# Block 2's heads: VectorE writes only the columns that change, and a head's norm is inverted with tokens in partitions

## The chip, the cores and the metric

The kernel runs as one program on one core of a Trainium2 chip. The metric is the device time of one execution in microseconds (us). Everything is computed in 32-bit floats. The engines are TensorE (PE in the views), VectorE (DVE), ScalarE (ACT) and SyncE (SP), which issues the weight transfers. Each runs its own instructions in order, and they wait for one another by semaphores.

## The reference

Two transformer blocks of width 2048 run over 256 tokens. The change is in the second block's two recurrent mixers, each with eight heads of width 128, over a chunked sequence of 512 tokens (256 context, 256 grid) in both directions:

```python
# _hgrn2, a gated linear attention, per head:
f = lb + (1.0 - lb) * jax.nn.sigmoid(fz);  key = (1.0 - lb) * jax.nn.sigmoid(-fz)
diff = bc[..., :, None, :] - bc[..., None, :, :]      # bc: running sum of log f
att = jnp.einsum('bhtk,bhsk,bhtsk->bhts', qc, kc, exp(diff) below the diagonal)
# _gated_deltanet, per head: a unit lower triangular system is solved
a = eye + jnp.where(strict, (kb @ kc.T) * decay, 0.0)
# both, per head, after the two directions are added:
o = _rmsnorm_2(o_f + _flip(o_b), norm_w) * gate
```

The root-mean-square norm of the last line runs over the 128 features of a token.

## The kernel before

Each mixer is a chain of eight heads. A head consists of a start, two strands (r = 0 forward, r = 1 backward) and an end, which adds the strands' outputs, takes the norm and applies the gate. Every part is written three times, as a generator for TensorE, VectorE and ScalarE, and each `yield` ends a phase. `lockstep` advances the strands together, so that all three engines run through the same phases; a head has 58 phases. The end of a head runs in the first phases of the next one. The chain of the forget heads (`forget_*`, names `hg`) starts eight phases after that of the delta heads (`delta_*`, names `dn`). `beside` spreads a background over these phases: eight groups of a projection whose matmuls (L592) keep TensorE busy. The order of each engine's instructions is therefore fixed by hand.

Both strands build a 128x128 triangular matrix out of seven levels. At level l the tokens lie in blocks of 2 x half with half = 128 >> (l + 1), and a level joins the first half of each block with the second.

- In `forget_vector` a level subtracts the running sums from their middle value (L1597 for first halves, L1598 for second ones), ScalarE takes the exponential of the whole 128x256 tile (L1654), VectorE multiplies by keys and queries (L1602, L1603), TensorE multiplies (L1510), and `copy_predicated` takes the masked elements of the 128x256 product over into `att` (L1608). Before the levels, the keys are a product (L1546) followed by one with a column (L1549).
- In `delta_vector` a level masks the matrix `nt` into `mt` (L1795, 128x512 for four token tiles). TensorE multiplies (L1710), ScalarE copies (L1847), TensorE multiplies the halves (L1717, L1719), and VectorE subtracts them in place (L1803, L1805, half-columns only).
- In a new delta head, `delta_tensor` writes rows of gates into banks 0 to 3 (L1685, L1687); L1767 on VectorE reads them. Bank 1 is also the one in which the end of the head before sums its squares (L1955).
- An end adds and squares (L1970 to L1972), TensorE sums the squares over the features with a matrix of ones (L1955), so that each token's sum stands in all 128 partitions; then the mean (L1975), the root on ScalarE (L1986), the reciprocal (L1978) and two products (L1979, L1980) are all 128x256.

Of the kernel before, what the change touches and what calls it, by code (L numbers as in the profile page):

```python
# [13 lines left out]
P = 128  # L14
# [234 lines left out]
class Kernel:  # L249
# [4 lines left out]
    def __init__(self, nc, io, known, pofs, cofs):  # L254
# [25 lines left out]
        self.arena = sb("arena", ARENA)  # L280
        masks = self.c("masks").rearrange("p (r l t) -> p r l t", r=2, l=7)
# [20 lines left out]
    def places(self):  # L302
# [47 lines left out]
        for r in range(2):  # L350
            self.hg.append(dict(f=a.take(4, P), k=a.take(4, P), e1=a.take(4, P), cum=a.take(4, P + 2), ks=a.take(4, P),
                                att=a.take(2, P), qe=a.take(2, P), lev=a.take(2, P), st=a.take(P), eend=a.take(4)))
        self.hvf, self.hvt = a.take(4, P), a.take(4, P)
        self.hq, self.hgt = ([a.take(2, P) for _ in range(2)] for _ in range(2))
# [8 lines left out]
        self.dzg = [self.mix[:, 3, :], self.mix[:, 4, :]]  # L363
        assert a.at <= ARENA - 1024, a.at
# [1116 lines left out]
def level_halves(x, half):  # L1481
    t = x.rearrange("p j (b two n) -> p j b two n", two=2, n=half)
    return t[:, :, :, 0, :], t[:, :, :, 1, :]
# [42 lines left out]
def forget_vector(k, r, head):  # L1526
# [62 lines left out]
    for level in range(7):  # L1589
        half = P >> (level + 1)  # L1590
        nb = P // (2 * half)
        mid = cm[:, 0:2, 0:P].rearrange("p j (b n) -> p j b n", n=2 * half)[:, :, :, half:half + 1].broadcast_to((P, 2, nb, half))
        c0, c1 = level_halves((after if fwd else before)[:, 0:2, :], half)
        m0, m1 = level_halves(m, half)
        k0, k1 = level_halves(kk[:, 0:2, :], half)
        q0, q1 = level_halves(k.hq[head % 2], half)
# [9 lines left out]
        mask = k.masks[r][:, level, :].unsqueeze(1).broadcast_to((P, 2, P)).bitcast(U32)  # L1606
# [14 lines left out]
def forget_scalar(k, r, head):  # L1621
# [51 lines left out]
def delta_tensor(k, r, head):  # L1673
# [7 lines left out]
    if head:  # L1681
        pe.wait_ge(*s.at("dn_o_mean", head - 1))
# [23 lines left out]
    for level in range(5, -1, -1):  # L1706
        yield
        pe.wait_ge(*s.at(*ev("masked", level)))
        for j in range(NT):
            mm = pe.matmul(b0[:, P * j:P * j + P], mt[:, j, :], x[:, j, :], start=True, stop=True)  # L1710
# [35 lines left out]
def delta_vector(k, r, head):  # L1746
# [15 lines left out]
    yield  # L1762
    yield
    yield
# [60 lines left out]
def delta_scalar(k, r, head):  # L1825
# [3 lines left out]
    yield  # L1829
    yield  # L1830
    yield
    yield
# [117 lines left out]
def end_tensor(k, name, head):  # L1950

    pe, s = k.nc.tensor, k.s
    bank, sq = (k.acc[3], k.hsq) if name == "hg" else (k.bank[1], k.dsq)
    pe.wait_ge(*s.at(name + "_o_sq", head))
    pe.matmul(bank[:, 0:T], k.c("ones"), sq, start=True, stop=True).then_inc(*s.made("tensor_done", name + "_o_sum", head))  # L1955
    yield
    yield

def end_vector(k, name, head):
# [15 lines left out]
    v.tensor_scalar(sq, bank[:, 0:T], 1.0 / P, 1e-6, ALU.mult, ALU.add).then_inc(*s.made("vector_done", name + "_o_mean", head))  # L1975
    yield
    v.wait_ge(*s.at(name + "_o_root", head))
    serial(k, v.reciprocal(sq, sq))  # L1978
    serial(k, v.scalar_tensor_tensor(o, o, w, sq, ALU.mult, ALU.mult))  # L1979
    v.tensor_tensor(dst, o, gate, ALU.mult).then_inc(*s.made("vector_done", name + "_end", head))  # L1980

def end_scalar(k, name, head):
    a, s, sq = k.nc.scalar, k.s, k.hsq if name == "hg" else k.dsq
    yield
    a.wait_ge(*s.at(name + "_o_mean", head))
    a.activation(sq, sq, ACT.Sqrt).then_inc(*s.made("scalar_done", name + "_o_root", head))  # L1986
# [24 lines left out]
def heads2_vector(k):  # L2011
# [12 lines left out]
    v.memset(k.ones_row, 1.0).then_inc(*s.made("vector_done"))  # L2024
    for r in range(2):
# [471 lines left out]
```

## Time and profile before

| what | value |
|---|---|
| median of 3 runs | 4655.85 us (4651.43 to 4659.77) |
| span of the profiled execution | 4650.0 us |
| block 2's heads in it | 2403 to 3284 us |
| busy in the span: TensorE, VectorE, ScalarE | 4321.8, 2756.5, 1602.9 us |
| mean granted TensorE clock | 0.961 |

### The profile page before, as it was taken

The numbers are of one execution on the slowest core, as the hardware profiler recorded it, in microseconds if no ns is written. First come the engines' busy times: TensorE is split into PE (matmuls) and PEld (weight loads), VectorE is DVE, ScalarE is ACT, GpSimd is POOL, SyncE is SP. The second block draws the span as 40 slices with busy tenths as digits, with TensorE's granted clock in tenths as the row PEclk, the third lists the DMA queues.
The fourth block names the chain that finished last, engine by engine and source line by source line (L and its number), as shares of the span: only waits on it lengthen the run. The fifth ranks groups of instructions, "written<-read, shape, count | busy, mean of one in ns | idle before, by whom it ended". The sixth has DMA issues, their size and how long they took to land.

```text
span 4650.0 us, 69801 instructions
## 1 busy us (share of the span) xinstructions
PE 4321.8 (93%) x28096; PEld 3686.2 (79%) x28096; DVE 2756.5 (59%) x5537; ACT 1602.9 (34%) x2841; POOL 0.2 (0%) x4
## 2 busy tenths in 40 slices
PE   8989997899999989999988989888899998999998
PEld 8433334899999978889778888888655898999998
DVE  5666664576566542234558877777533666655654
ACT  4121112454444432234123333333100444444443
POOL 0000000000000000000000000000000000000000
PEclk9989998999999999999899999999988999999999
DMA  6744454466666544457451222121522654656653
GB/s 187 246 138 143 143 173 135 151 187 190 187 182 190 187 134 123 115 144 212 128 156 56 60 65 62 54 65 46 156 76 77 200 190 131 191 187 186 186 189 129
DMA packets 383296, 669.52 MB, mean 144 GB/s; under 512 B 44009, under 2 KB 77642, under 8 KB 382460
## 3 DMA queue, kind: packets, MB, share of 16 engines
q1 hardware_dynamic: 329280, 597.83, 42.8%
q10 hardware_dynamic: 53692, 67.22, 4.4%
q8 instruction: 221, 3.62, 0.3%
q14 instruction: 103, 0.84, 0.1%
HBM read 634.87 MB, written 29.46 MB: 143 GB/s over the span
## 4 chain that ended last, share of the span: by engine, by line
PE 64%; DVE 13%; ACT 3%; issue 3%; DMA 1%; ACTq 0%; DVEq 0%
PE acc L550 13%; PE acc L552 13%; PE acc L551 13%; PE acc L592 8%; PE bank L550 2%; PE bank L552 2%; PE bank L551 2%; ACT weights_hi L514 1%; PE bank L2193 1%; PE bank L1719 1%; PE bank L1710 1%; PE bank L1717 1%; DVE arena L1544 1%; PE acc L1510 1%; DVE arena L676 1%
## 5 line engine op out<-in xcount | busy, mean ns | idle before, releaser
L529 DVE TENSOR_TENSOR weights_lo<-weights_ring,weights_hi 128x512 fp32r<-128x512 f32 x1600 | 1093.6, 691 | 1019.4 <-ACT weights_hi L514 1017.7
L514 ACT ACTIVATE weights_hi<-weights_ring 128x512 fp32r<-128x512 f32 x1600 | 992.8, 629 | 1076.4 <-PE acc L552 879.9
L551 PE MATMUL acc<-arena_halves,weights_hi 128*128 128x256 f32 (+2 forms) x3136 | 914.2, 292 | 0.0
L550 PE MATMUL acc<-arena_halves,weights_lo 128*128 128x256 f32 (+1 forms) x2944 | 861.6, 293 | 21.2 <-DVE weights_lo L529 12.3
L552 PE MATMUL acc<-arena_halves,weights_hi 128*128 128x256 f32 (+1 forms) x2944 | 859.9, 292 | 0.0
L550 PE MATMUL acc<-moving_halves,weights_lo 128*128 128x256 f32 (+1 forms) x2816 | 790.4, 281 | 68.4 <-DVE weights_lo L529 67.8
L552 PE MATMUL acc<-moving_halves,weights_hi 128*128 128x256 f32 (+1 forms) x2816 | 785.1, 279 | 0.0
L551 PE MATMUL acc<-moving_halves,weights_hi 128*128 128x256 f32 x2624 | 729.7, 278 | 0.0
L592 PE MATMUL acc<-moving,weights_ring 128*128 128x256 f32 x2304 | 588.1, 401 | 21.8 <-ACT arena L695 11.1
L551 PEld LDWEIGHTS acc<-arena_halves,weights_hi 128*128 128x128 f32 x3136 | 590.1, 188 | 13.5
L550 PEld LDWEIGHTS acc<-moving_halves,weights_lo 128*128 128x128 f32 x2816 | 533.7, 190 | 76.8 <-DVE weights_lo L529 48.9
L550 PEld LDWEIGHTS acc<-arena_halves,weights_lo 128*128 128x128 f32 x2944 | 553.5, 188 | 34.3 <-DVE weights_lo L529 13.1
L552 PEld LDWEIGHTS acc<-arena_halves,weights_hi 128*128 128x128 f32 x2944 | 554.1, 188 | 14.2
L552 PEld LDWEIGHTS acc<-moving_halves,weights_hi 128*128 128x128 f32 x2816 | 533.6, 189 | 0.0
L592 PEld LDWEIGHTS acc<-moving,weights_ring 128*128 128x128 f32 x2304 | 444.3, 202 | 108.3 <-issue 37.6
L551 PEld LDWEIGHTS acc<-moving_halves,weights_hi 128*128 128x128 f32 x2624 | 496.8, 189 | 0.0
L1144 PE MATMUL acc<-weights_ring,cc 128*2 128x512 f32 x768 | 352.0, 600 | 2.8 <-DMA weights_ring<-in_w_ada 2.8
L1144 PEld LDWEIGHTS acc<-weights_ring,cc 128*2 128x2 f32 x768 | 56.9, 85 | 238.3 <-issue 225.3
L551 PE MATMUL bank<-arena_halves,weights_hi 128*128 128x256 f32 (+2 forms) x640 | 208.0, 325 | 0.0
L550 PE MATMUL bank<-arena_halves,weights_lo 128*128 128x512 f32 (+1 forms) x512 | 172.3, 337 | 0.0
L552 PE MATMUL bank<-arena_halves,weights_hi 128*128 128x512 f32 (+1 forms) x512 | 171.8, 336 | 0.0
L1710 PE MATMUL bank<-arena 128*128 128x128 f32 x768 | 113.0, 302 | 28.9 <-DVE arena L1795 28.7
(422 smaller groups left out, 4815.5 us busy)
## 6 DMA issues: line engine op xcount, KB each, us to landing
weights_ring<-in_w_in SPq DMA_DIRECT2D x624, 256.0 KB, 2.7
weights_ring<-in_w_ff SPq DMA_DIRECT2D x512, 256.0 KB, 3.0
weights_ring<-in_w_ada SPq DMA_DIRECT2D x384, 256.0 KB, 3.0
weights_ring<-in_w_up SPq DMA_DIRECT2D x256, 256.0 KB, 3.0
weights_ring<-in_w_down SPq DMA_DIRECT2D x256, 256.0 KB, 3.2
weights_ring<-in_w_out SPq DMA_DIRECT2D x128, 256.0 KB, 3.2
weights_ring<-in_w_branch SPq DMA_DIRECT2D x96, 256.0 KB, 3.3
s_state<-arena ACTq DMA_DIRECT2D x36, 256.0 KB, 3.0
```

The lines of the kernel that those rows point to most:

```text
L514: a.activation(whi, k.slot(g.ring0 + kc), ACT.Copy).then_inc(*s.made("scalar_done", "high", n))
L529: v.tensor_tensor(wlo, k.slot(g.ring0 + kc), whi.bitcast(F32), ALU.subtract).then_inc(*s.made("vector_done", "low", n))
L550: pe.matmul(g.out[m], wlo[:, cols], xhi, start=first, stop=False, skip_group_check=g.shared)
L551: pe.matmul(g.out[m], whi[:, cols], xlo, start=False, stop=False, skip_group_check=g.shared)
L552: mm = pe.matmul(g.out[m], whi[:, cols], xhi, start=False, stop=last, skip_group_check=g.shared)
L592: mm = pe.matmul(g.out[m], k.slot(g.ring0 + kc)[:, m * P:(m + 1) * P], g.x(kc), start=kc == 0 and m % 2 == 0, stop=last, skip_group_check= ...
L676: v.tensor_scalar(tmp, g.out[m], 0.0, None, ALU.max, ALU.bypass).then_inc(*s.made("vector_done", "relu", g.name, g.index, m))
L1144: mm = pe.matmul(g.out[0], ccv[:, kc, :], k.slot(g.ring0 + kc), start=kc == 0, stop=kc == g.kchunks - 1)
L1510: mm = pe.matmul(po[:, P * j:P * j + P], h["lev"][:, j, :], h["lev"][:, j, :], start=True, stop=True)
L1544: own(v.reciprocal(f[:, j, :], f[:, j, :]))
L1710: mm = pe.matmul(b0[:, P * j:P * j + P], mt[:, j, :], x[:, j, :], start=True, stop=True)
L1717: pe.matmul(b0[:, 64 * j:64 * j + 64], xt[:, j, :], level_columns(y[:, j, :], level, r), start=True, stop=True)
```

## The change

- Delta masks: levels 5 to 0 each get a tile of their own (`mts`, twelve in all, for both strands), zeroed once by a memset, and the product with the mask writes only the columns that the mask can set: 128x256 instead of 128x512. Seven of the tiles are new memory (`level_own`, zeroed at the program's start), five lie in a buffer that is free in this stage (`level_mix`, zeroed just before the heads).
- Forget levels: both halves of a block are subtracted in one instruction, both are multiplied in one (`keys_and_queries` views keys and queries as one operand, for which the query buffers were moved), the sign goes into ScalarE's exponential, which is now one instruction for each half, and the predicated copy takes only the half-columns that can change.
- Keys: the column goes into the first product.
- Norm: the sum of squares is taken with the tokens in partitions, as one column for each token tile; mean, root and reciprocal are 128x2; then VectorE makes a diagonal matrix of them and TensorE spreads it to all partitions (`o_spread`), from where the first product reads it in the bank. An end has a phase more.
- `delta_tensor` therefore waits in all heads but the first for the end of the head before (`dn_end`) instead of for its mean, and the delta strands of these heads start one phase later.

```diff
+        self.level_own = sb("level_masks", 7, 512)
...
+            if r:
+                self.hq_at = a.at
+                self.hq = [a.take(2, P) for _ in range(2)]
...
+        self.o_cols = {"hg": a.take(2), "dn": a.take(2)}
...
+        self.level_mix = [self.mix[:, 5 + 2 * i:7 + 2 * i, :].rearrange("p a b -> p (a b)") for i in range(5)]
...
+    v.memset(k.level_own[:, :, :], 0.0).then_inc(*s.made("vector_done"))
...
+def half_columns(x, half):
+
+    t = x.rearrange("p j t -> p (j t)").rearrange("p (c two n) -> p two c n", two=2, n=half)
+    return t, t[:, 0, :, :], t[:, 1, :, :]
+
+def keys_and_queries(k, r, head, half):
+
+    keys, queries = k.hg[r]["k_at"], k.hq_at + 2 * P * (head % 2)
+    first, second = (keys, queries + half) if r == 0 else (queries, keys + half)
+    apart = second - first
+    t = k.arena[:, first:first + 2 * apart].rearrange("p (two d) -> p two d", two=2)[:, :, 0:2 * P]
+    return t.rearrange("p two (c q n) -> p two c q n", q=2, n=half)[:, :, :, 0, :]
+
+def of_second(x, half, second):
+    return x.rearrange("p j (b two n) -> p j b two n", two=2, n=half)[:, :, :, second, :]
...
-    own(v.tensor_tensor(kk, e1, f, ALU.mult))
+    own(v.scalar_tensor_tensor(kk, e1, lb1c, f, ALU.mult, ALU.mult))
...
-    own(v.tensor_scalar(kk, kk, lb1c, None, ALU.mult, ALU.bypass))
...
-        own(v.tensor_tensor(m0, mid, c0, ALU.subtract))
-        own(v.tensor_tensor(m1, c1, mid, ALU.subtract), *ev("spans", level))
+        both, m0, m1 = half_columns(m, half)
+        own(v.tensor_tensor(blocks(m), blocks(sums), mid, ALU.subtract), *ev("spans", level))
...
-        own(v.tensor_tensor(m0, m0, k0 if fwd else q0, ALU.mult))
-        own(v.tensor_tensor(m1, m1, q1 if fwd else k1, ALU.mult), *ev("level", level))
+        own(v.tensor_tensor(both, both, keys_and_queries(k, r, head, half), ALU.mult), *ev("level", level))
...
-        own(v.copy_predicated(att, mask, tiles(po, 2)), *(ev("att") if level == 6 else ()))
+        own(v.copy_predicated(of_second(att, half, 1 - r), mask, of_second(tiles(po, 2), half, 1 - r)), *(ev("att") if level == 6 else ()))
...
-        a.activation(h["lev"], h["lev"], ACT.Exp).then_inc(*s.made("scalar_done", *ev("span_decays", level)))
+        _, m0, m1 = half_columns(h["lev"], P >> (level + 1))
+        a.activation(m0, m0, ACT.Exp, scale=-1.0).then_inc(*s.made("scalar_done"))
+        a.activation(m1, m1, ACT.Exp).then_inc(*s.made("scalar_done", *ev("span_decays", level)))
...
     if head:
-        pe.wait_ge(*s.at("dn_o_mean", head - 1))
+        yield
+        pe.wait_ge(*s.at("dn_end", head - 1))
...
-        own(v.tensor_tensor(mt, nt, k.masks[r][:, level, :].unsqueeze(1).broadcast_to((P, NT, P)), ALU.mult), *ev("masked", level))
+        mask = level_columns(k.masks[r][:, level, :], level, 1 - r).unsqueeze(1).broadcast_to((P, NT, 1 << level, half))
+        own(v.tensor_tensor(of_second(d["mts"][level], half, 1 - r), of_second(nt, half, 1 - r), mask, ALU.mult), *ev("masked", level))
...
-    pe.matmul(bank[:, 0:T], k.c("ones"), sq, start=True, stop=True).then_inc(*s.made("tensor_done", name + "_o_sum", head))
-    yield
+    for j in range(2):
+        mm = pe.matmul(bank[:, j:j + 1], sq[:, P * j:P * j + P], k.c("ones")[:, 0:1], start=True, stop=True)
+    mm.then_inc(*s.made("tensor_done", name + "_o_sum", head))
+    yield
+    yield
+    pe.wait_ge(*s.at(name + "_o_diagonal", head))
+    for j in range(2):
+        mm = pe.matmul(bank[:, P * j:P * j + P], k.c("ones"), sq[:, P * j:P * j + P], start=True, stop=True)
+    mm.then_inc(*s.made("tensor_done", name + "_o_spread", head))
...
-    serial(k, v.reciprocal(sq, sq))
-    serial(k, v.scalar_tensor_tensor(o, o, w, sq, ALU.mult, ALU.mult))
+    serial(k, v.reciprocal(col, col))
+    v.tensor_tensor(sq.rearrange("p (j t) -> p j t", j=2), k.ident.unsqueeze(1).broadcast_to((P, 2, P)),
+                    col.unsqueeze(2).broadcast_to((P, 2, P)), ALU.mult).then_inc(*s.made("vector_done", name + "_o_diagonal", head))
+    yield
+    v.wait_ge(*s.at(name + "_o_spread", head))
+    serial(k, v.scalar_tensor_tensor(o, o, w, bank[:, 0:T], ALU.mult, ALU.mult))
...
+    for part in k.level_mix:
+        v.memset(part, 0.0).then_inc(*s.made("vector_done"))
...
-        nc = bacc.Bacc("TRN2", target_bir_lowering=False, num_devices=1)
+        nc = bacc.Bacc("TRN2", target_bir_lowering=False, num_devices=1, dynamic_dma_scratch_size=2048)
```

## Rows read from the trace of the kernel before

**Rows 1.** Busy time by stretch: the heads, then the two halves of one head.
```profile
core 0: us, PE busy (x) PEld busy (x) DVE busy (x) ACT busy (x) POOL busy (x), PEclk, DMA share, GB/s
2403.00:3284.00 881.00, 778.45 (x5226) 717.72 (x5227) 692.15 (x1792) 307.06 (x617) 0.00 (x0) 0.93 0.21 61
2628.00:2663.00 35.00, 28.40 (x193) 25.34 (x191) 33.99 (x65) 12.38 (x21) 0.00 (x0) 0.94 0.11 31
2664.00:2695.00 31.00, 31.00 (x224) 29.77 (x222) 21.77 (x57) 10.53 (x21) 0.00 (x0) 0.91 0.24 68
```
**Rows 2.** Chain that ended last, in the heads: start us, us, engine, line.
```profile
2429.12 0.69 DVE arena L1795
...
2443.21 0.40 DVE arena L1549
...
2507.26 0.44 DVE arena L1608
...
2535.03 1.76 DVE arena L1978
...
2663.42 3.79 PE bank L1710 x16
...
2675.32 1.79 PE bank L1710 x16
...
3204.92 0.71 DVE arena L1795
...
3264.00 0.48 DVE arena L1608 x2
...
3277.12 1.76 DVE arena L1978
```
**Rows 3.** Groups of VectorE in the heads: count, busy us, mean ns, idle before.
```profile
L1795 DVE TENSOR_TENSOR arena<-arena,consts_sb 128x512 f32<-128x512 f32 x96 | 66.4, 692 | 3.3
...
L1805 DVE TENSOR_TENSOR arena<-arena,bank 128x256 f32<-128x256 f32 x96 | 39.8, 415 | 11.0 <-PE bank L1719 11.0
...
L1549 DVE TENSOR_SCALAR arena<-arena 128x512 f32<-128x512 f32 x16 | 7.7, 480 | 0.0
...
L1979 DVE SCALAR_TENSOR_TENSOR mixed<-mixed,params_sb 128x256 f32<-128x256 f32 x8 | 3.9, 485 | 0.3
```
**Rows 4.** Timeline of VectorE where instructions follow one another: start, us.
```profile
2567.34 0.42 DVE L1581 TENSOR_TENSOR arena<-arena 128x256 f32<-128x256 f32 x1
2567.68 0.99 DVE L1585 TENSOR_TENSOR arena<-arena 128x256 f32<-128x256 f32 x2
...
2571.19 0.28 DVE L1597 TENSOR_TENSOR arena<-arena 128x128 f32<-128x128 f32 x1
2571.39 0.28 DVE L1598 TENSOR_TENSOR arena<-arena 128x128 f32<-128x128 f32 x1
```
**Rows 5.** Chain at the boundary of two delta heads, twice.
```profile
2620.08 0.34 DVE mixed L1975
...
2620.47 2.07 PE bank L1685 x8
...
2625.51 0.89 PE bank L1687 x8
...
2728.56 0.34 DVE mixed L1975
...
2733.74 1.04 DVE arena L1767 x4
```
**Rows 6.** Groups of ScalarE and VectorE that price the new small instructions.
```profile
L1654 ACT ACTIVATE arena<-arena 128x256 f32<-128x256 f32 x112 | 43.3, 413 | 99.5 <-DVE arena L1598 99.5
...
L1770 DVE TENSOR_TENSOR arena<-arena 128x4 f32<-128x4 f32 x16 | 2.6, 162 | 0.6
...
L2252 DVE MEMSET arena<- 1x512 f32 x4 | 1.9, 485 | 0.6 <-DVE arena L2250 0.6
```
**Rows 7.** Timeline: VectorE's first instruction of the program.
```profile
25.61 0.44 DVE L749 TENSOR_SCALAR rstd<-bank 128x272 f32<-128x272 f32 x1 [25.61 <-PE bank L742]
```

More of the change, by code:

```diff
@@ L363, in places @@
         self.dzg = [self.mix[:, 3, :], self.mix[:, 4, :]]
+        self.level_mix = [self.mix[:, 5 + 2 * i:7 + 2 * i, :].rearrange("p a b -> p (a b)") for i in range(5)]
+        mt = [self.level_own[:, i, :] for i in range(7)] + self.level_mix
+        for r in range(2):
+            self.dn[r]["mts"] = [mt[6 * r + level].rearrange("p (j t) -> p j t", j=4) for level in range(6)]
         assert a.at <= ARENA - 1024, a.at
@@ L1479, in hg_views @@
     return h, cm[:, :, 1:P + 1], cm[:, :, 0:P], cm[:, :, P:P + 1]
-def level_halves(x, half):
-    t = x.rearrange("p j (b two n) -> p j b two n", two=2, n=half)
-    return t[:, :, :, 0, :], t[:, :, :, 1, :]
+def half_columns(x, half):
[9 more added lines that the diff above has]
+    return x.rearrange("p j (b two n) -> p j b two n", two=2, n=half)[:, :, :, second, :]
 def forget_tensor(k, r, head):
@@ L1591, in forget_vector @@
         nb = P // (2 * half)
[L1592 to L1596, printed above, removed]
-        own(v.tensor_tensor(m0, mid, c0, ALU.subtract))
-        own(v.tensor_tensor(m1, c1, mid, ALU.subtract), *ev("spans", level))
+        blocks = lambda x: x.rearrange("p j (b n) -> p j b n", n=2 * half)
+        mid = blocks(cm[:, 0:2, 0:P])[:, :, :, half:half + 1].broadcast_to((P, 2, nb, 2 * half))
+        sums = (after if fwd else before)[:, 0:2, :]
+        both, m0, m1 = half_columns(m, half)
+        own(v.tensor_tensor(blocks(m), blocks(sums), mid, ALU.subtract), *ev("spans", level))
         yield
@@ L1709, in delta_tensor @@
         for j in range(NT):
-            mm = pe.matmul(b0[:, P * j:P * j + P], mt[:, j, :], x[:, j, :], start=True, stop=True)
+            mm = pe.matmul(b0[:, P * j:P * j + P], d["mts"][level][:, j, :], x[:, j, :], start=True, stop=True)
         mm.then_inc(*s.made("tensor_done", *ev("left", level)))
@@ L1761, in delta_vector @@
     own(copy(k, mt, col(be)), *ev("spread"))
-    yield
-    yield
-    yield
+    for _ in range(4 if head else 3):
+        yield
     v.wait_ge(*s.at(*ev("rows")))
@@ L1794, in delta_vector @@
         v.wait_ge(*own.last)
-        own(v.tensor_tensor(mt, nt, k.masks[r][:, level, :].unsqueeze(1).broadcast_to((P, NT, P)), ALU.mult), *ev("masked", level))
+        half = P >> (level + 1)
+        mask = level_columns(k.masks[r][:, level, :], level, 1 - r).unsqueeze(1).broadcast_to((P, NT, 1 << level, half))
+        own(v.tensor_tensor(of_second(d["mts"][level], half, 1 - r), of_second(nt, half, 1 - r), mask, ALU.mult), *ev("masked", level))
         yield
@@ L1828, in delta_scalar @@
     ev = lambda name, *x: ("dn_" + name, r, head, *x)
[L1829 to L1832, printed above, removed]
+    for _ in range(5 if head else 4):
+        yield
     a.wait_ge(*s.at(*ev("logs")))
@@ L1974, in end_vector @@
     v.wait_ge(*s.at(name + "_o_sum", head))
-    v.tensor_scalar(sq, bank[:, 0:T], 1.0 / P, 1e-6, ALU.mult, ALU.add).then_inc(*s.made("vector_done", name + "_o_mean", head))
+    col = k.o_cols[name]
+    v.tensor_scalar(col, bank[:, 0:2], 1.0 / P, 1e-6, ALU.mult, ALU.add).then_inc(*s.made("vector_done", name + "_o_mean", head))
     yield
     v.wait_ge(*s.at(name + "_o_root", head))
-    serial(k, v.reciprocal(sq, sq))
-    serial(k, v.scalar_tensor_tensor(o, o, w, sq, ALU.mult, ALU.mult))
+    serial(k, v.reciprocal(col, col))
+    v.tensor_tensor(sq.rearrange("p (j t) -> p j t", j=2), k.ident.unsqueeze(1).broadcast_to((P, 2, P)),
+                    col.unsqueeze(2).broadcast_to((P, 2, P)), ALU.mult).then_inc(*s.made("vector_done", name + "_o_diagonal", head))
+    yield
+    v.wait_ge(*s.at(name + "_o_spread", head))
+    serial(k, v.scalar_tensor_tensor(o, o, w, bank[:, 0:T], ALU.mult, ALU.mult))
     v.tensor_tensor(dst, o, gate, ALU.mult).then_inc(*s.made("vector_done", name + "_end", head))
 def end_scalar(k, name, head):
-    a, s, sq = k.nc.scalar, k.s, k.hsq if name == "hg" else k.dsq
+    a, s, col = k.nc.scalar, k.s, k.o_cols[name]
     yield
     a.wait_ge(*s.at(name + "_o_mean", head))
-    a.activation(sq, sq, ACT.Sqrt).then_inc(*s.made("scalar_done", name + "_o_root", head))
+    a.activation(col, col, ACT.Sqrt).then_inc(*s.made("scalar_done", name + "_o_root", head))
     yield
```

6 lines of the change are left out of this document (3 added, 3 removed).

## The prediction

> **What bounds the kernel now.** I read the time by stretch first, then the chain that ended last, then the groups of VectorE instructions, then the timeline where one head follows another. Block 2's heads take 881 of the 4650 us, and in them the granted TensorE clock is lower than 1 on average [rows 1]. The reader should see two halves in a head. In 2628 to 2663 VectorE is busy 33.99 of 35 us and TensorE 28.40. In 2664 to 2695 TensorE is busy all of the time and VectorE 21.77 of 31 us [rows 1]. The chain says the same: in the first half each VectorE instruction stands behind the one before, from 2663.42 on TensorE's matmuls follow one another [rows 2]. Added up over the 1892 pieces of the whole stage, from which [rows 2] are taken, the chain has 372 us of VectorE, 445 us of TensorE and 27 us of ScalarE. So a VectorE instruction made shorter pays where the chain runs over it, and nowhere else. TensorE's own work in its half is untouched.
>
> **The price of a VectorE instruction.** On the chain a following, independent instruction starts before the one ahead has ended: two 128x128 products of 0.28 us start 0.20 us apart, two of 128x256 start 0.34 us apart (2567.34 and 2567.68) [rows 4]. So two of 128x128 merged into one of 128x256 save 0.40 - 0.34 = 0.06 us of the engine, not 2 x 0.28 - 0.42 = 0.14. One of 128x512 cut to 128x256 saves 0.69 - 0.42 = 0.27 us, waited for or not [rows 3, 4]. Strides don't cost: L1805 reads and writes the same half-columns, of every level, at 415 ns [rows 3].
>
> **Part 1, delta masks (L1795).** 96 products of 128x512 become 128x256. The chain runs over 52 of them (34.0 us, first and last in [rows 2]). 52 x 0.27 = 14.0 us saved. The other 44 lie beside TensorE's work: 0.
>
> **Part 2, keys (L1549).** All 16 lie on the chain from 2443.21 on, 0.40 us each, by pace and not by their duration of 480 ns [rows 2, 3]. The product that takes the column in has a scalar read from memory; L1979, with such a scalar, takes 485 ns for 256 columns, L1581 without it 0.42 us [rows 3, 4]. 16 x 0.34 = 5.4 us saved.
>
> **Part 3, the levels of the forget heads.** 112 levels: two subtractions and two products each merge, and the predicated copy (L1608) goes from 256 to 128 columns. The copies on the chain are 17 pieces, about 24 copies, in 7.4 us [rows 2]; the halved one I put at 0.31 (0.44 less the 0.14 that lies between 0.28 and 0.42 [rows 4]): 24 x 0.13 = 3.2 us. About eight merged pairs on the chain give 0.06 each, 0.5 us. ScalarE's exponential goes from one of 128x256 (413 ns [rows 6]) to two of 128x128. Bounds from its rows: nothing more, or a second full 413 ns. Its back-to-back starts are closer than its durations, as on VectorE, so I take 0.10 us. It lies on the chain four times: 0.4 us lost. Elsewhere ScalarE, busy a third of the stage [rows 1], hides it; were that cover gone, 112 x 0.10 = 11 us. Net 3.3 us.
>
> The Trainium skill, page Advanced Engine Details and Errata, section The Read-Write Bubble, says that on ScalarE and VectorE latency stands exposed between instructions, so that many small ones cost more than one large one. It speaks for the merged pairs and against the split exponential. [rows 4] show for VectorE that part of that latency is overlapped when nothing is waited for. By the rule taken fully, merging would save 0.14 and splitting lose about 0.2 us, and on these few places of the chain the sum would move by under 1 us.
>
> **Part 4, the norm.** 16 ends. Removed: a 1.76 us reciprocal and a 0.34 us mean of 128x256, and 0.2 us of ScalarE's root. Added: the same on 128x2 (a 128x4 instruction takes 0.16 us [rows 6]), a 128x256 product with the identity (0.42), and a trip to TensorE and back. For the forget ends the trip has a phase of other VectorE work over it; nothing waits at once for that end. The chain runs over five of their reciprocals. Gross 1.76 + 0.34 + 0.42 - 0.16 - 0.2 - 0.2 - 0.36 = 1.6 us. In the middle heads ScalarE's table loads and copies, and L1717 behind them, follow within about 1.5 us, so I take 1.0; the last two ends, with nothing else to run, are priced with their matmuls at 0.9 each. 4 x 1.0 + 2 x 0.9, and a few tenths for the others: 6.5 us.
>
> **Part 5, the boundary between delta heads.** TensorE must write the new head's rows (L1685, L1687) into the bank in which the norm now lives for longer: it waits for the head's end instead of the mean. Queued behind that wait are everything else on TensorE, background projection too. VectorE waits for the rows at L1767. Before, the rows ran under the reciprocal. From the mean's start to the second strand's L1767: 2728.56 to 2733.74, 5.2 us, at full clock; 2620.08 to 2626.40, 6.3 us, with the rows at half clock [rows 5]. After: mean 0.16, root 0.2, reciprocal 0.2, diagonal 0.42, two matmuls 0.6 (four follow one another in 0.89 at 2625.51, and the first has its fill of some 0.15 before it), two products 0.48 and 0.42, handovers 0.3: 2.8 us, and only then the rows, 3.7 us at full clock, 5.9 as at 2620.47, 7.2 if all of it runs at half clock. So 6.5, 8.7 or 10.0 us: a loss of 1.3, 2.4 or 3.7 us for each of seven boundaries. In this trace three were fast and four slow. I take 3 x 1.3 + 4 x 2.4 = 14 us lost, bounds 9 (all fast) and 26 (all at half clock). The reciprocal's saving is already in it.
>
> **Part 6, the rest.** Five memsets of 128x512 come before the first head, where VectorE has just been released by ScalarE and the first rows wait for it. A 512-column memset took 485 ns [rows 6]: 2.4 us lost. The large memset at the program's start lies under the 25.61 us in which VectorE first waits for TensorE [rows 7]: 0. Extra matmuls, 0.4 us for each of 16 ends, fall where TensorE has room: 0, or 7 us if not. The moved buffers and the DMA scratch size add no instruction: 0.
>
> **Sum.** 14.0 + 5.4 + 3.3 + 6.5 = 29 us saved; 14 + 2.4 = 16 us lost. Net 13 us: the profiled span of 4650.0 becomes 4637. The median of the runs, 4655.85, is 5.9 above that span, so 4643. A difference under 0.2%, 9 us, can hardly be told from none.
>
> **Rivals.**
> - *A, the clock comes back.* At a mean grant of 0.93, with levels of 1.2 and 2.4 GHz, about 14% of the stage, 123 us, runs at half clock. At 2663.42 sixteen records take 3.79 us instead of 1.79 [rows 2], right after a stretch in which TensorE was idle. A shorter first half packs TensorE's same work denser. If most such dips vanish, up to 25 us more: 4643 - 25 = 4618, with fast boundaries 4613. Against it: a new idle place at the boundary. The Trainium skill, page TensorE: Matmul & The Clock Gate, section Part 1, says that activity releases the throttle; these rows agree.
> - *B, what is saved is given back.* TensorE, at 81% in 2628 to 2663 [rows 1], or ScalarE becomes the one waited for, so that half of part 1 is lost (7 us), or all boundaries run at half clock (12 us more). That gives 4650 or 4655, both together 4662: no change.
> - *C, slower by the boundary.* TensorE now idles at two places within some 6 us: before the spreading matmuls and before the rows. If that leaves it at half clock in every boundary and on through the next products, the loss is 3.7 us of part 5 and the dearer matmuls up to L1703, another 3 us: 6.7 x 7 = 47 us against 29 - 2.4 = 27 saved, 4676. It decides from a loss of 36 / 7 = 5.1 us a boundary. For it: four of seven boundaries are already slow. Against: after the rows VectorE sets the pace, under which slow matmuls are partly hidden.
>
> **Chances.** Forecast (4630 to 4655) 0.46, A 0.24, B 0.19, C 0.11. Taking the part of the forecast and of B under 4646.5 as faster: faster 0.61, same 0.28, slower 0.11. The range leaves out the ends of A and most of C: 4612 to 4662.
>
> **What would show it.** L1795's successor at 0.42 us and fewer of its pieces on the chain; the small reciprocal near 0.2 us; TensorE idle for 2 to 3 us before each later L1685, and VectorE idle for 1 to 2 us before L1767; a first half of a head some 4 us shorter and a second half unchanged. I'm wrong if the level steps of TensorE's half get shorter too, if ScalarE's split exponentials come on to the chain, or if the mean clock of the stage moves by more than 0.02.

## The result: slower by 0.9%

The kernel after takes 4698.15 us (median of 4 runs, 4685.42 to 4705.38), beside 4653.64 us for the kernel before in the same series (4 runs). The ratio is 1.0088, 95% interval 1.0068 to 1.0108. The forecast was 4643 us. The profiled execution has a span of 4704.0 us (before 4650.0) and a mean granted clock of 0.957 (before 0.961). One execution of e13 (below) took 8939.64 us at a mean granted clock of 0.632 and is left out of every comparison.

Busy time by stretch, kernel after. Start and end, length, then busy us of TensorE, its weight loads, VectorE, ScalarE and GpSimd, each with its count, the granted clock, DMA:

```profile
0.00:2403.00 2403.00, 2258.75 (x13612) 1798.63 (x13612) 1295.54 (x2405) 802.64 (x1356) 0.20 (x4) 0.97 0.55 165
2403.00:3330.00 927.00, 792.61 (x5320) 731.80 (x5321) 620.05 (x1573) 314.60 (x732) 0.00 (x0) 0.92 0.21 59
```

The heads now end at about 3327 us and not 3280. That is 47 of the 54 us between the two spans. The rest of the program takes 1377 us in this execution and took 1370 before; in the other kernels' profiled executions, which don't change it, it takes 1369 to 1378. VectorE's busy time in the stage fell from 692 us [rows 1] to 620: the work was taken away as planned. Added up over the chain that ended last in the stage, VectorE's part fell from 372 to 319 us, and TensorE's rose from 440 (the prediction has 445) to 545. What left one engine's account came back, and more, on the other's.

Groups of VectorE in the heads, kernel after (count, busy us, mean ns of one, idle before and its releaser). The first two lines answer to L1795 in [rows 3], the last is the product that took in L1549; L1825 is the other half of the pair whose second is L1805 there:

```profile
L1817 DVE TENSOR_TENSOR level_masks<-arena,consts_sb 128x256 f32<-128x256 f32 x56 | 23.8, 425 | 1.9
L1817 DVE TENSOR_TENSOR mixed<-arena,consts_sb 128x256 f32<-128x256 f32 x40 | 17.0, 425 | 1.4
L1621 DVE TENSOR_TENSOR arena<-arena 128x256 f32<-128x256 f32 x112 | 45.4, 424 | 22.1 <-ACT arena L1674 22.1
L1626 DVE COPY_PREDICATED arena<-consts_sb,acc 128x128 f32<-128x128 uint32 x112 | 37.9, 339 | 99.0 <-PE acc L1532 95.1
L1825 DVE TENSOR_TENSOR arena<-arena,bank 128x256 f32<-128x256 f32 x80 | 33.3, 416 | 55.0 <-PE bank L1740 55.0
L1812 DVE TENSOR_TENSOR arena<-consts_sb,bank 128x512 f32<-128x512 f32 x16 | 11.0, 685 | 12.2 <-PE bank L1724 12.1
L1568 DVE SCALAR_TENSOR_TENSOR arena<-arena 128x512 f32<-128x512 f32 x16 | 12.0, 752 | 0.6
```

The mask costs what it was priced at: 425 ns, where 692 was before. The last column, the idle time before the instruction, holds the news. The predicated copy waits 95 us for TensorE (63 before), L1825 55 us (25 for the same form before), and L1812, which waited for nothing before, 12 us. All waits of VectorE for TensorE in the stage sum to 239 us, 141 before.

**The boundary between delta heads** looks as it was forecast for a slow one. Timeline, kernel after, with what each instruction waited for:

```profile
2859.40 0.15 DVE L2003 TENSOR_SCALAR arena<-bank 128x2 f32<-128x2 f32 x1
2860.05 0.42 DVE L2007 TENSOR_TENSOR mixed<-consts_sb,arena 128x256 f32<-128x256 f32 x1
2860.53 1.23 PE L1982 MATMUL bank<-mixed,consts_sb 128*128 128x128 f32 x4 [1.87 <-DVE mixed L2007]
2862.31 0.42 DVE L2012 TENSOR_TENSOR moving<-mixed 128x256 f32<-128x256 f32 x1
2862.79 2.07 PE L1706 MATMUL bank<-consts_sb,arena 128*128 128x128 f32 x8 [0.18 <-DVE moving L2012]
2866.61 1.13 DVE L1787 TENSOR_SCALAR arena<-bank,arena 128x128 f32<-128x128 f32 x4 [3.36 <-PE bank L1708]
2868.39 1.12 DVE L1787 TENSOR_SCALAR arena<-bank,arena 128x128 f32<-128x128 f32 x4 [0.40 <-PE bank L1708]
```

The rows (L1706, L1685 before) start behind the end's last product and run at half clock, 2.07 us for eight records as in [rows 5]. From the mean to the second strand's L1787 it is 9.0 us; the forecast had 8.7 for a boundary whose rows run at half clock. This is the longest of the seven. They take 6.8 to 9.0 us, 8.0 on average, where they took 5.2 to 6.5, 5.7 on average, in the kernel before. So this is a real loss, 16 us in all, but no place for the 47 us by which the heads got longer.

**What lies elsewhere** shows 50 us further on. Timeline, kernel after, level 3 of a delta head:

```profile
2908.42 1.16 PE L1731 MATMUL bank<-arena,mixed 128*128 128x128 f32 x8
2909.78 0.63 ACT L1655 ACTIVATE arena<-arena 128x512 f32<-128x512 f32 x1 [4.67 <-DVE arena L1592]
2911.52 1.06 ACT L1867 ACTIVATE arena<-bank 128x512 f32<-128x512 f32 x2
2912.15 1.10 PE L1738 MATMUL bank<-arena 128*128 128x64 f32 x8 [1.71 <-ACT arena L1867]
2915.47 1.91 PE L1740 MATMUL bank<-arena 128*128 128x64 f32 x8
2917.42 0.42 DVE L1825 TENSOR_TENSOR arena<-arena,bank 128x256 f32<-128x256 f32 x1 [2.02 <-PE bank L1740]
```

ScalarE is idle for 4.67 us, waiting for VectorE's sums in the forget strands (L1655). The delta strands' copy L1867 stands behind it in the same queue; the first strand's matmuls that it reads (L1731) had ended at 2908.5 us, 3 us before the copy starts. TensorE needs that copy and is idle for 1.71 us. VectorE then waits for TensorE. In the kernel after without the shift (e3 below) the order on ScalarE is the other one, and the copies L1866 (L1867 above) wait for their own matmuls alone:

```profile
2877.44 0.60 ACT L1866 ACTIVATE arena<-bank 128x512 f32<-128x512 f32 x1 [2.12 <-PE bank L1730]
2879.14 0.60 ACT L1866 ACTIVATE arena<-bank 128x512 f32<-128x512 f32 x1 [1.11 <-PE bank L1730]
2879.76 1.28 ACT L1655 ACT_TABLE_LOAD   x1
2881.05 0.63 ACT L1655 ACTIVATE arena<-arena 128x512 f32<-128x512 f32 x1
```

And another place, on TensorE:

```profile
2879.73 0.71 PE L1976 MATMUL acc<-consts_sb,arena 128*128 128x1 f32 x4 [3.11 <-DVE arena L1999]
2880.30 1.09 PE L1936 MATMUL acc<-consts_sb,arena 128*128 128x128 f32 x4
2881.18 3.06 PE L1724 MATMUL bank<-consts_sb,arena 128*128 128x128 f32 x16
2883.13 0.69 DVE L1812 TENSOR_TENSOR arena<-consts_sb,bank 128x512 f32<-128x512 f32 x1 [2.17 <-PE bank L1724]
```

The left product of level 6 (L1724, "left 6" from here on) stands behind the sum of squares of a forget head's end (L1976), which waits for VectorE. In the kernel before, and in e3, both (the copy of level 3 and left 6) were ahead of these neighbours. They changed places because the delta strands run one phase later than the forget strands beside them.

The clock falls at both places. Stretches of the kernel after (columns as in the first view, the granted clock is the third number from the end):

```profile
2878.00:2879.70 1.70, 0.00 (x0) 0.00 (x0) 1.63 (x5) 0.00 (x0) 0.00 (x0) 1.00 0.34 125
2881.00:2882.00 1.00, 1.00 (x6) 1.00 (x5) 0.00 (x0) 1.00 (x1) 0.00 (x0) 0.50 0.00 0
2912.00:2913.00 1.00, 0.85 (x8) 0.85 (x8) 0.34 (x1) 0.59 (x2) 0.00 (x0) 1.00 0.00 0
2915.00:2916.00 1.00, 1.00 (x7) 1.00 (x6) 0.40 (x1) 0.00 (x0) 0.00 (x0) 0.50 0.00 0
```

At left 6 TensorE has been idle for 3.11 us and is at half clock (0.50) soon after it starts again: sixteen records of L1724 take 3.06 us, where eight take 1.06 in e3. At level 3 it still runs two groups of eight at full clock after its pause (1.10 us for L1738) and is at half clock from about 2914.3 us on, so that the last eight take 1.91.

Waits in the heads, kernel after (engine and line, what it waited for: us in total, times, longest). The first is the largest of all, but ScalarE has time for it; the other three belong to the two places above:

```profile
ACT arena L1867 <- PE bank L1731: 197.1, 71, 10.0
ACT arena L1655 <- DVE arena L1592: 32.2, 7, 4.7
PE acc L1976 <- DVE arena L1999: 22.6, 8, 4.0
PE bank L1738 <- ACT arena L1867: 11.2, 8, 1.7
```

### The profile page after: what moved, and what is told of

Same layout as the page of the kernel before. It is cut to its first block, busy times and chain, and to the rows that moved or that the text cites. A ratio compares the mean times of both kernels' runs of the same rounds, so it can differ in the third digit from the quotient of the medians.

```text
span 4704.0 us, 69887 instructions
## 1 busy us (share of the span) xinstructions
PE 4344.5 (92%) x28192; PEld 3707.0 (79%) x28192; DVE 2687.4 (57%) x5319; ACT 1609.8 (34%) x2953; POOL 0.2 (0%) x4
## 4 chain that ended last, share of the span: by engine, by line
PE 65%; DVE 12%; ACT 3%; issue 3%; DMA 1%; ACTq 0%; DVEq 0%
PE acc L559 13%; PE acc L561 13%; PE acc L560 13%; PE acc L601 8%; PE bank L560 2%; PE bank L559 2%; PE bank L561 2%; PE bank L1731 1%; ACT weights_hi L523 1%; DVE arena L1566 1%; PE bank L2227 1%; PE bank L1740 1%; PE bank L1738 1%; PE acc L1532 1%; DVE arena L685 1%
## 5 line engine op out<-in xcount | busy, mean ns | idle before, releaser
L560 PEld LDWEIGHTS bank<-arena_halves,weights_hi 128*128 128x128 f32 x640 | 120.3, 188 | 9.6
```

What stands on the lines that cost most here:

```text
L560: pe.matmul(g.out[m], whi[:, cols], xlo, start=False, stop=False, skip_group_check=g.shared)
```

## The experiments

Each ratio is to the kernel before, timed beside it on the same chip, with its 95% interval. "Shift" is the extra phase of the delta strands in heads 1 to 7. "Steps" are mean times between landmarks of a delta head in the timeline of VectorE, over heads 1 to 7. The landmarks are VectorE's first instruction on the first strand's products (L1802), left 6 (L1812) and each level's result (L1827). The "period" is the mean distance of two heads from head 1 to head 7.

### First: which part

**e1_no_norm**: the kernel after with the old norm, the old wait and no shift; what is left are masks, keys, levels, memsets.

```diff
-        yield
-        pe.wait_ge(*s.at("dn_end", head - 1))
+        pe.wait_ge(*s.at("dn_o_mean", head - 1))
```

> The changed kernel with the old norm, the old wait for the head's mean and without the extra phase: only masks, levels, keys and memsets are changed. Theory (the loss of the change is all in the norm's end and in what it moves): parts 1 to 3 give what was forecast, 23 us, less 2.4 for the memsets, so 4653.6 - 20 = 4633 us (4625 to 4642). Rival (the levels themselves cost, by ScalarE's split exponential and the waits for it): 4655 us or more.

0.9967 [0.9953, 0.9981], 4638.3 us beside 4655.1: 15 us saved (9 to 22 by the interval), forecast 20.

**e2_norm_only**: the kernel before with the new norm, its wait and the shift.

> The kernel before with nothing but the new norm, the wait for the head's end and the extra phase. Theory: it carries the whole loss, 44 + 20 = 64 us, so about 4718 us (4700 to 4730). Rival (levels cost): the norm carries only the 7 x 2.5 us of its boundaries, about 4665 us.

1.0135 [1.0117, 1.0154], 4720.7 us, as forecast. All of the loss comes with the norm, its wait and the shift.

**e3_no_shift**: the kernel after; the one edit is that the shift goes (TensorE's `yield` ahead of the wait for `dn_end`, and its counterparts on VectorE and ScalarE). The wait stays.

> The changed kernel without the extra phase of the delta strands (the wait for the head's end stays; the strands of the two chains stand to one another as before). Theory S (the shift puts the delta matmuls L1724 behind the forget end's sum in TensorE's queue, and VectorE waits for them at L1812, and later steps pair up worse): 7 boundaries give back 4 us each, about 4670 us (4660 to 4680). Theory W (the loss is the wait itself: TensorE stands still until the head's end, and the clock with it): no gain, 4690 to 4705 us.

0.9993 [0.998, 1.0007], 4651.8 us. The shift alone turns this into 1.0088: some 44 to 46 us, the whole loss, and more than the 28 us that the expectation gave it. The period is 113.9 us after, 107.6 here and 107.9 before. The wait at left 6 is gone, and that behind the levels is 30 us where it was 25 before and 55 after (L1811 and L1824 here are L1812 and L1825 after):

```profile
L1811 DVE TENSOR_TENSOR arena<-consts_sb,bank 128x512 f32<-128x512 f32 x16 | 10.9, 679 | 0.0
L1824 DVE TENSOR_TENSOR arena<-arena,bank 128x256 f32<-128x256 f32 x80 | 33.0, 412 | 30.4 <-PE bank L1739 30.3
```

**e4_hg_norm**: new norm for the forget heads only; delta heads have the old norm and wait, and no shift.

> The changed kernel with the new norm for the forget heads alone; the delta heads have the old norm, the old wait and no extra phase. Both theories: as without the norm, less 6 us for the reciprocals on the chain, about 4627 us (4620 to 4637). Rival (a trip to TensorE and back costs wherever it stands, since it holds up the matmuls queued behind it): 4640 us or more.

0.9938 [0.9926, 0.995], 4626.8 us: the fastest kernel of the study. Busy time in its heads (columns as above):

```profile
2403.00:3256.00 853.00, 759.77 (x5283) 701.83 (x5284) 625.10 (x1564) 313.70 (x729) 0.00 (x0) 0.96 0.22 64
```

The heads end at 3248 us and not at 3280, and the clock in them is 0.96, not 0.93 [rows 1]. From e1 to e4 the forget heads' norm saves 0.29%, 13 us (11 by the medians). From e4 to e3 the delta heads' norm with its wait costs 0.55%, 25 us, 3.6 us a boundary. The timelines say the same: from the mean to the second strand's rows it is 8.9 us on average in e3 (7.1 to 10.5) and 5.3 in e4 (5.2 to 6.0).

### Second: the shift alone, and where in a head it hurts

**e5_shift_only**: the kernel before with nothing but the shift.

```diff
     if head:
+        yield
         pe.wait_ge(*s.at("dn_o_mean", head - 1))
```

> The kernel before with nothing but the extra phase of the delta strands in heads 1 to 7 (old norm, old wait, old masks). Theory S: the extra phase is what costs, whatever stands around it: e3 against the changed kernel gives 46 us, so about 4700 us (4690 to 4710). Rival P (the phase costs only where it adds to the new norm's trips): under 4670 us.

1.0117 [1.0102, 1.0132], 4710.2 us, 53 us lost. No part of the new arithmetic is needed for the loss.

**e6_delay_nine**: the kernel after, the forget chain starting nine phases after the delta chain, not eight.

```diff
-    chains = [chain(k, "hg", hg_start, forget, end, 8), chain(k, "dn", dn_start, delta, end)]
+    chains = [chain(k, "hg", hg_start, forget, end, 9), chain(k, "dn", dn_start, delta, end)]
```

> The changed kernel with the forget chain nine phases behind the delta chain instead of eight, so that from head 1 on both chains stand to one another as before the change; the extra phase of the delta strands stays. Theory S1 (the pairing of the two chains' steps in one phase is what costs): the 46 us come back, 4650 to 4660 us. Rival S2 (the phase is lost inside the delta chain itself, between its end and its rows): no gain, 4690 to 4705 us.

0.9975 [0.9966, 0.9984], 4642.7 us. The shift is still there, and the loss is gone, and the steps to left 6 and from level 3 to level 2 are 6.7 and 8.2 us, as in e3 (6.7 and 8.3). So the loss lies in how the steps of the two chains pair up, not in a phase more.

The next four runs are the kernel after with the extra phase at another place. **e7_shift_early** gives the phase back before left 6; **e8_shift_late** begins it there; **e9_shift_level_five** begins it behind left 6; **e10_shift_level_two** behind level 3. For e10, on each engine:

```diff
+        if head and level == 2:
+            yield
```

> The changed kernel, where the delta strands give their extra phase back before the first inverse step: rows, decays and products stand one phase later, all levels stand where they did. Theory S1 with the pairing of the levels and of L1724 behind the forget end's sum as the cost: 4650 to 4660 us. If the pairing of rows and products with the forget chain's last steps costs instead: 4690 us or more. In between: both.

1.0008 [0.9999, 1.0017]: the levels stand where they did, and nearly all of the loss is gone.

> The complement: no extra phase at the rows, but one before the first inverse step, so that only that step and the levels stand one phase later. If the levels' pairing costs: about 4690 to 4700 us. If the rows' and products' pairing costs: 4650 to 4660 us.

1.0112 [1.0099, 1.0125]: all of the loss.

> As the late shift (4709), but the extra phase stands after the first inverse step, so that this step (L1724) is again ahead of the forget end's sum in TensorE's queue and only levels 5 to 0 come one phase later. The landmarks of the traces put 2.3 us a head on that step and 4 to 5 us on the levels. Theory Q (three separate queue orders add up): 4709 - 7 x 2.3 = 4693 us (4685 to 4700). Rival (it all hangs on that first step, the rest follows from its delay): 4650 to 4660 us.

1.0095 [1.0082, 1.0109], 4696 us: nearly all of it, as the theory of separate queue orders had it.

> The extra phase stands between levels 3 and 2, so that ScalarE's copy of level 3 is issued where it was without a shift, ahead of the forget strands' exponential of their sums (which waits for VectorE's scans), and only levels 2 to 0 and the end come later. Theory Q: 4652 us as without any shift, plus up to 1 us a head for the last levels: 4650 to 4662 us. Rival (any extra phase anywhere costs about 7 us a head): 4700 us.

1.0014 [1.0005, 1.0023]. Beside e3 (0.9993), a phase later costs some 7 us for the rows and products at the start of a head (e7; the intervals of e7 and e3 still meet), and some 10 for levels 2 to 0 (e10). Nearly all of the loss comes up between left 6 and level 3. The places don't add up exactly: begun at left 6 (e8) the shift costs more than begun at the start.

**e16_shift_level_three** was run later, with the phase between levels 4 and 3.

> The kernel after with the extra phase given between level 4 and level 3 of the delta strands and not at their start. With the phase before level 5 it took 1.0095 of the kernel before, with the phase behind level 3 only 1.0014. Queue theory (ScalarE's copy of level 3 behind the exponential of sums is the largest place): most of the 38 us between these two, at least 22 us, is still there: 1.006 to 1.009, 4680 to 4694. Rival, the loss is spread evenly over the levels 5, 4 and 3 that run in other phases: two thirds of it go: about 1.004, 4670.

1.0071 [1.0056, 1.0086]. From e16 to e10 is 0.57%, 27 us: level 3 alone. Levels 5 and 4 have 11 us (e9 to e16) and left 6 about 8 (e8 to e9), but for both the intervals of the two runs meet. "Spread evenly" is out.

The steps show where the time goes (us; the step from level 2 to level 1 is 8.4 in all of them):

| step | e3, no shift | after | e9 | e16 | e13 (below) |
|---|---|---|---|---|---|
| products to left 6 | 6.7 | 8.8 | 6.7 | 6.7 | 9.2 |
| left 6 to level 5 | 11.4 | 13.2 | 13.8 | 11.4 | 13.3 |
| level 5 to 4 | 10.4 | 10.2 | 10.1 | 10.4 | 10.0 |
| level 4 to 3 | 8.9 | 8.3 | 8.7 | 11.8 | 7.5 |
| level 3 to 2 | 8.3 | 11.7 | 12.3 | 9.2 | 8.4 |
| level 1 to 0 | 6.1 | 7.1 | 7.1 | 7.1 | 7.1 |

In e9 left 6 has its old place and its old 6.7 us, and yet e9 is no faster than the kernel after (1.0095 beside 1.0088): the next step and the one behind level 3 got longer in its place. So the 2 us a head at left 6 can't be counted as a part of the loss that comes back by itself.

### Third: small checks

**e11_masks_only**: masks on half columns and the memsets, on the kernel before.

> The kernel before with the delta masks on half the columns and the memsets, nothing else of the change. By the prediction's parts 1 and 6: 14.0 - 2.4 = 11.6 us saved, 4644 us (4638 to 4650). Rival (what parts 2 and 3 brought is the whole gain of e1, 16 us, and TensorE sets the pace under the masks): 4652 us or more.

0.9981 [0.9972, 0.9991]: 9 us saved (4 to 13 by the interval, which holds the forecast 11.6).

**e12_hg_norm_delay_nine**: e4 with a delay of nine.

> The fastest kernel so far (new norm for the forget heads alone, 4627) with the forget chain nine phases behind instead of eight: the opposite misalignment of that which cost 46 us. Theory Q (queue orders at three places, each on one side only): the delta steps stand further ahead of the forget steps, so nothing of that kind arises, 4622 to 4637 us. Rival (the eight phases are a tuned optimum, and a step to either side costs): 4650 us or more.

0.9984 [0.9975, 0.9994], 4643.0 us; by the ratios 0.46%, 21 us, more than e4 (16 by the medians, which were taken on two chips). A step to the other side costs too. Which pair it is was not found: its head is slower in several small steps.

### Fourth: the queues themselves

**e13_sums_exp_later**: the kernel after, shift kept. ScalarE alone issues L1655 and L1656 one phase later, so that L1867 of level 3 is ahead of them again. The other engines' order is the same.

```diff
     yield
+    yield
     a.wait_ge(*s.at(*ev("sums")))
     a.activation(h["ks"], h["ks"], ACT.Exp).then_inc(*s.made("scalar_done"))
     a.activation(h["eend"], h["cum"][:, :, P], ACT.Exp).then_inc(*s.made("scalar_done", *ev("decays")))
     yield
     yield
-    yield
```

> The kernel after, shift kept, with one edit: ScalarE issues the exponential of the forget strands' sums one phase later, so the delta strands' copy of level 3 is again ahead of it in ScalarE's queue. Nothing else moves on any engine. Queue theory: the step from level 3 to level 2 (11.7 us after, 8.3 without the shift) comes back to about 8.3 to 9; 7 heads x 3 us = 21 us and a higher granted clock behind it: about 4675 to 4680, ratio 1.0045 to 1.006, against 1.0088 for the kernel after. Rival, the shift costs because whole stretches of VectorE and TensorE work of the two chains now lie on one another, not because of single places in a queue: then this edit brings at most 5 us or loses a little, since VectorE's keys wait later: 4693 or more.

1.005 [1.0032, 1.0068], 4676.0 us, as forecast. ScalarE's timeline at the same place of the same head; L1655 and L1656 are now L1656 and L1657:

```profile
2905.90 0.60 ACT L1867 ACTIVATE arena<-bank 128x512 f32<-128x512 f32 x1 [4.42 <-PE bank L1731]
2907.02 0.60 ACT L1867 ACTIVATE arena<-bank 128x512 f32<-128x512 f32 x1 [0.53 <-PE bank L1731]
2907.64 1.28 ACT L1656 ACT_TABLE_LOAD   x1
2908.93 0.63 ACT L1656 ACTIVATE arena<-arena 128x512 f32<-128x512 f32 x1
```

and in its waits:

```profile
DVE arena L1825 <- PE bank L1740: 31.9, 32, 2.7
```

The copy waits for its own matmuls and for nothing else, by the time that the exponential is issued VectorE's sums are there, and L1825's wait goes from 55.0 to 31.9 us, nearly the 30.3 of e3. The step from level 3 to level 2 is 8.4 us: 11.7 after, 8.3 without the shift. The period falls from 113.9 to 111.6 us, 16 us over seven heads; the medians say 22, the ratios 18. So the place of one pair of exponentials in one queue is the largest single part of the loss that a run gave back.

**e14_forget_sum_later**: TensorE alone issues L1976 of the forget ends one phase later, behind L1936 and L1724. **e15_both_later**: e13 and e14 together.

> The kernel after, shift kept, with one edit: TensorE issues the two-column sum of squares at the end of a forget head one phase later, behind the transposes and behind the delta strands' left product of level 6. Queue theory: the step from products to left 6 (8.8 to 9.2 us after, 6.7 without the shift) comes back, perhaps also the 1.9 us of the next step: 7 x 2.3 = 16 to 7 x 4.2 = 29 us: 4669 to 4682, ratio 1.003 to 1.006. Rival of overlapping stretches: 5 us at most, 4693 or more.

1.0121 [1.0106, 1.0137], 4705.7 us; the queue theory had 1.003 to 1.006.

> Both edits of the two runs before on the kernel after, shift kept. Queue theory: 37 to 50 us of the 46 that the shift cost come back: 4648 to 4661, ratio 0.999 to 1.0015, as without the shift (4652). Rival of overlapping stretches: 10 us at most, 4688 or more. Were only one of the two places real, it comes out as the better of the two runs before.

1.0077 [1.0063, 1.0091], 4687.0 us; the theory had 0.999 to 1.0015. Both are about 0.3% worse than without the edit of e14. In e14 the wait of L1812 is gone, and a new one stands in its place. Its row in the groups, kernel e14:

```profile
L1812 DVE TENSOR_TENSOR arena<-consts_sb,bank 128x512 f32<-128x512 f32 x16 | 10.9, 678 | 0.0
```

and in its waits:

```profile
DVE arena L2006 <- PE acc L1978: 27.6, 7, 4.8
```

L2006 is the mean (L2003 in the kernel after); it is ahead of L1812 in VectorE's queue and now waits for the late sum.

**e17_forget_end_later**: the whole end of a forget head one phase later on all engines. **e18_end_and_exp_later**: with the edit of e13.

> The kernel after, shift kept, with the whole end of a forget head one phase later on all three engines (not its sum on TensorE alone, which turned the wait at left 6 into a wait of VectorE's mean for the sum, 27.6 us in seven heads, and came out at 1.0121). Queue theory: left 6 is no longer behind the sum, and the mean no longer ahead of left 6's product on VectorE: the step from products to left 6 goes from 8.8 to about 6.7 us and no new wait comes: 7 x 2.3 = 16 us off 4698: 4682, ratio 1.0055 (1.004 to 1.007). Rival: the work of the end, 1.3 us of VectorE, has to lie somewhere in the first half, where VectorE is the bound, so the place is not worth anything: 1.008 to 1.010.

1.0091 [1.0077, 1.0105], in the rival's range.

> Whole end of a forget head one phase later and the exponential of sums one phase later on ScalarE, shift kept. The exponential alone brought the ratio from 1.0088 to 1.0050. Queue theory: both places add up: 4677 - 16 = 4661, ratio 1.0015 (1.0005 to 1.003), nearly as without the shift. Rival: only the exponential counts: 1.004 to 1.006.

1.0057 [1.0041, 1.0073], in the rival's range too. Neither differs from its partner (1.0088 and 1.005). But these two did not remove the wait that they aimed at. Timeline of e18 at left 6:

```profile
2883.51 0.42 DVE L1999 TENSOR_TENSOR arena<-arena 128x256 f32<-128x256 f32 x1
...
2884.08 1.09 PE L1936 MATMUL acc<-consts_sb,arena 128*128 128x128 f32 x4 [3.88 <-DVE arena L1999]
...
2884.96 3.03 PE L1724 MATMUL bank<-consts_sb,arena 128*128 128x128 f32 x16
```

The transposes of the next head's values (L1936) wait for the forget end as well (`hg_o_sq`), and they stand ahead of L1724. With the sum moved away, they took over its wait. So the rival (the place is worth nothing) is not shown either. Transposes moved behind left 6 were not tried.

## Why the prediction was wrong

**The step that failed** is one that the prediction doesn't have. "One phase later" is named in front of it and in no term of the sum; the prediction says that TensorE's own work in its half is untouched and expects the second half of a head unchanged. Where a step moves, all that it issues counts; here everything that the delta strands issue in seven heads moved against everything of the forget strands, on three queues. It was read as a change of position without work, hence without cost. It costs 44 to 46 us on this kernel and 53 on the kernel before. Of these, 16 to 22 us are one exchange on ScalarE: behind it the step from level 3 to level 2 goes from 8.3 to 11.7 us, and back to 8.4 when it is undone (e13). The other 25 or so are located but not explained. Against the kernel without the shift, e13 still loses 2.5 us a head ahead of left 6, 1.9 behind it and 1.0 at level 0, and gains 1.9 at levels 4 and 3. That the first is the wait at L1936 and L1976 fits the timeline and stays open.

How much of the loss is the clock isn't separated. An estimate from the traces: in the heads the mean granted clock is 0.943 in e3 and 0.923 after, which is 99 and 143 us at half clock. The 44 us more would be 22 us of lost time if TensorE were busy in all of them. At the two places shown above the clock fell behind a wait that the shift brought, so this is most likely a share of the same 46 us and not another cause.

**Parts 1 to 3 and the memsets** gave 15 of 20 us, and the masks with the memsets 9 of 12 (e11). Both forecasts lie inside the intervals, so the masks' term stands. One term of part 3 doesn't: the halved predicated copy, put at 0.31 us each.

```profile
2933.02 0.74 DVE L1626 COPY_PREDICATED arena<-consts_sb,acc 128x128 f32<-128x128 uint32 x2 [2.13 <-PE acc L1532]
2855.39 0.89 DVE L1626 COPY_PREDICATED arena<-consts_sb,acc 128x128 f32<-128x128 uint32 x2 [0.38 <-PE acc L1532]
```

The first row is of level 0: two copies of 0.30 us, between which VectorE waits 0.15 for TensorE (80 of the 112 copies, levels 0 to 4, take 0.29 or 0.30). The second is of the last level. In levels 5 and 6, where the columns taken over lie in pieces of two and of one, all 32 copies take 0.44, as one of 256 columns did in [rows 2]. And the copies on the chain are just those of levels 5 and 6: 7.41 us of them before, 7.36 after. The 3.2 us for them were not there. "Strides don't cost" was read from L1805 and doesn't hold for this instruction. The prediction also counted about 24 copies in 7.4 us; 8 of these 24 pieces last 0.04 us or less, so there are 16.

**Part 4**, the forget heads' norm, was too small: 11 to 13 us for the forget heads alone, against 6.5. The 1.6 us gross a head was cut to 1.0 for table loads and copies that would follow at once. 13 / 8 = 1.6 and 11 / 8 = 1.4: little of it was lost. The stage's clock rises with it, from 0.944 in e1 to 0.963 in e4, so a part of the gain may be the clock.

**Part 5**, the boundary: right in mechanism and place, 25 us against 14. The price of the new boundary was right: 8.9 us on average in e3, where 8.7 was forecast with the rows at half clock, and in six of e3's seven boundaries the first eight records take 2.07 us. What it must be compared with was mis-sized. Five of the seven old boundaries in e4 are fast, 5.2 us, and the mean is 5.3, so each costs 3.6 and not 1.3 or 2.4. (In the trace before, four were fast and three slow, not three and four.) That the sum meets the bound of 26, "half clock all through", is a coincidence: 10.0 us a boundary was not the rule.

**Part 6**: the memset at the start is hidden (VectorE's next instruction starts at 25 us), the five before the heads take 485 ns each, as said.

Without the shift the measured parts are -15 - 13 + 25 = -3 us, which is e3's 0.9993 (it must be, since they are differences between e1, e4 and e3). So the forecast of 13 us saved would have been off by 10 even then, inside its range; the shift put it outside.

**The rivals.** A (the clock comes back, 4618) comes nearest to e4: 4627 us at 0.96. But e4 keeps the old boundary. The Trainium skill, page TensorE: Matmul & The Clock Gate, section Part 1, says that activity releases the throttle; the rows agree from the other side, since the clock falls to 0.50 at left 6 and at level 3 behind pauses of 3.11 and 1.71 us, at once or some 2 us later. C (slower by the boundary, 4676) has the right sign and nearly the size, for the wrong reason, which is luck: with the boundary wait alone, e3 is no slower than before. Its threshold of 5.1 us a boundary was not reached (3.6). B did not occur as such. Of the three signs that the prediction named for being wrong, none showed clearly: the level steps of TensorE's half got longer and not shorter, the mean clock of the stage moved by 0.01 (0.934 to 0.923), and the split exponentials are on the chain with 3.1 us where the whole one had 1.7. The signs were drawn up for other failures than the one that came.

## What to carry to other kernels

Where the order of all engines is written by hand in common phases, a phase added to one of two interleaved chains may be the most expensive part of an edit, as it was here: list, for each engine, which instruction now stands behind which, and what the one in front waits for. If a step needs a phase more, give it where nothing pairs up (e7: 1.0008), or move the other chain along (e6: 0.9975 where the kernel after has 1.0088, by one number in the code). And when a wait is to be freed by moving what stands ahead, look at everything between the two in the queue: the next instruction may carry the same wait (L1936).

## What the hardware showed that was not expected

- A predicated copy of 128x128 from a bank takes 0.29 or 0.30 us where its columns lie in pieces of 4 to 64, and 0.44 where they lie in pieces of two or one, as much as one of 128x256. The 339 ns in the list of groups is the mean of the two.
- A pair of one-column matmuls over 128 rows (four records at L1976) holds TensorE for 0.47 us to the start of the next instruction in 12 of 16 cases. A pair with 128 columns (four records at L1718) holds it for 0.45. One column costs what 128 do.
- The shift alone moved the mean granted clock of the whole program from 0.962 (e3) to 0.957, that of the heads from 0.94 to 0.92.
